# Second joint attention: the samples' decay as one 32 by 128 product for each row group, ahead of the key products

## What is computed

```python
def _fox_attend(q, k, v, cq, ck, qpos, kpos):
    scores = jnp.einsum('bthd,bshd->bhts', q, k).astype(jnp.float32) * SCALE
    scores = scores + jnp.moveaxis(cq, 1, 2)[..., :, None] - jnp.moveaxis(ck, 1, 2)[..., None, :]
    mask = kpos[None, :] <= qpos[:, None]
    p = jax.nn.softmax(jnp.where(mask, scores, NEG_INF), axis=-1)
    return jnp.einsum('bhts,bshd->bthd', p.astype(v.dtype), v)
...
    c_all = jnp.cumsum(logf_all, axis=1)
```

## Time and profile before

| | us |
|---|---|
| median of 3 runs | 3663.12 |
| lowest and highest run | 3660.04, 3667.07 |
| time of the profiled execution | 3663.1 |
| its span, first to last instruction | 3661.3 |
| TensorE matmuls busy in it | 3400.0 |
| mean granted clock of TensorE | 0.967 |

### The profile page before, as it was taken

How to read it: one execution, slowest core, us unless ns; L and a number is a source line. 1 busy time by engine, 2 the same in 40 slices (tenths; PEclk the granted TensorE clock), 3 DMA queues, 4 the chain that set the end, 5 groups by cost and what they waited for, 6 DMA issues and landing times. The chain is left out here.

```text
span 3661.3 us, 62984 instructions
## 1 busy us (share of the span) xinstructions
PE 3400.0 (93%) x25000; PEld 2909.1 (79%) x25000; DVE 1601.0 (44%) x2913; ACT 1123.9 (31%) x2343; POOL 254.6 (7%) x338
## 2 busy tenths in 40 slices
PE   8998699798999999997899799999988999999997
PEld 7876466577999999996789756666567999999996
DVE  5417477463333333335231276666533333333334
ACT  4215255443212112113222145555433121211211
POOL 2310000032000000004000000000013000000003
PEclk9999799999999999998999999999988999999999
DMA  5435598443111111112554498889543111111102
GB/s 171 124 126 182 191 325 320 154 155 115 35 34 57 34 46 34 39 41 92 149 175 126 139 362 310 314 314 319 198 167 121 46 34 34 57 34 46 34 30 102
DMA packets 398384, 493.21 MB, mean 135 GB/s; under 512 B 68464, under 2 KB 250256, under 8 KB 398032
## 3 DMA queue, kind: packets, MB, share of 16 engines
q1 hardware_dynamic: 398176, 490.35, 40.3%
HBM read 407.10 MB, written 84.10 MB: 134 GB/s over the span
## 5 line engine op out<-in xcount | busy, mean ns | idle before, releaser
L2546 DVE TENSOR_TENSOR f_gated<-f_gated,f_up 128x384 f32<-128x384 f32 x132 | 73.1, 554 | 736.1 <-ACT f_gated L2476 736.1
L2570 DVE TENSOR_TENSOR f_y<-f_y,f_down 128x512 f32<-128x512 f32 x396 | 269.5, 686 | 229.4 <-PE f_down L2665 229.3
L2652 PE MATMUL f_gate<-m_ht_hi,f_w_hi 128*128 128x384 f32 x1056 | 355.5, 337 | 12.1 <-DVE f_w_lo L2597 12.1
L2652 PE MATMUL f_gate<-m_ht_lo,f_w_hi 128*128 128x384 f32 x1056 | 355.0, 336 | 0.0
L2652 PE MATMUL f_gate<-m_ht_hi,f_w_lo 128*128 128x384 f32 x1056 | 354.9, 336 | 0.0
L2652 PE MATMUL f_up<-m_ht_hi,f_w_lo 128*128 128x384 f32 x1056 | 352.7, 334 | 0.0
L2652 PE MATMUL f_up<-m_ht_hi,f_w_hi 128*128 128x384 f32 x1056 | 352.7, 334 | 0.0
L2652 PE MATMUL f_up<-m_ht_lo,f_w_hi 128*128 128x384 f32 x1056 | 352.7, 334 | 0.0
L2665 PE MATMUL f_down<-f_wo_hi,f_act_hi 128*128 128x512 f32 x792 | 313.8, 396 | 10.5 <-DVE f_y L2570 9.2
L2665 PE MATMUL f_down<-f_wo_lo,f_act_hi 128*128 128x512 f32 x792 | 309.9, 391 | 0.0
L2665 PE MATMUL f_down<-f_wo_hi,f_act_lo 128*128 128x512 f32 x792 | 309.7, 391 | 0.0
(11 more groups left out here) (396 smaller groups left out, 6677.1 us busy)
## 6 DMA issues: line engine op xcount, KB each, us to landing
jc_kc<-in_cache_c_k SPq DMA_DIRECT2D x64, 1024.0 KB, 10.2
jc_vc<-in_cache_c_v SPq DMA_DIRECT2D x64, 1024.0 KB, 8.8
jb_kc<-in_cache_b_k SPq DMA_DIRECT2D x32, 1024.0 KB, 10.7
jb_vc<-in_cache_b_v SPq DMA_DIRECT2D x32, 1024.0 KB, 9.3
m_raw<-in_w_ffn_in SPq DMA_DIRECT2D x44, 512.0 KB
f_raw<-in_w_ffn_in SPq DMA_DIRECT2D x44, 512.0 KB
f_raw_o<-in_w_ffn_out SPq DMA_DIRECT2D x22, 1024.0 KB, 6.4
m_raw<-x SPq DMA_DIRECT2D x18, 512.0 KB, 4.1
```

The lines of the kernel that those rows point to most:

```text
L2546: dve.tensor_tensor(prod[:, b], silu[:, b], up[:, q, 0:gw], ALU.mult).then_inc(prod_done, 1)
L2570: dve.tensor_tensor(part, part, down[:, half, :], ALU.add).then_inc(added, 1)
L2652: last = pe.matmul(acc[:, q, 0:gw], a[:, s, k, u, :], b[:, k, token], start=(k == 0 and j == 0), stop=(k == KT - 1 and j == 2))
```

## The change

In jc the five products of each tile become four, and ahead of them stands one product for each row group that writes all 128 partitions of its PSUM bank at once, with all of `select` for that row group as weights (32 rows by 128 columns) and the same 512 decays. It starts the accumulation (`start=True`), and the key products of jc no longer do. For jb (`diff` is true) nothing changes.

```diff
--- before.py
+++ after.py
@@ -1536,18 +1536,19 @@
                     if u:
                         pe.wait_ge(scaled, u)
                 pe.wait_ge(s_copied, 4 * u + 2 * pair)
-                for step in range(4 if diff else 5):
+                if not diff:
+                    for a in (2 * pair, 2 * pair + 1):
+                        rows_a = slice(Q * a, Q * a + Q)
+                        pe.matmul(s_ps[:, a % 2], select[rows_a], bias[rows_a, u % 2, 0:bank], start=True, stop=False,
+                                  skip_group_check=True, tile_position=(Q * a, 0))
+                for step in range(4):
                     for c in range(4):
                         for a in (2 * pair, 2 * pair + 1):
                             rows_a, hb = slice(Q * a, Q * a + Q), 4 * c + step
-                            if step < 4:
-                                weights = q_blocks[rows_a, hb // 2, hb % 2]
-                                moving = kc[rows_a, u % 2, 0:parts * per, Q * hb:Q * hb + Q]
-                            else:
-                                weights = select[rows_a, Q * c:Q * c + Q]
-                                moving = bias[rows_a, u % 2, 0:bank].rearrange("p (t r) -> p t r", r=Q)
+                            weights = q_blocks[rows_a, hb // 2, hb % 2]
+                            moving = kc[rows_a, u % 2, 0:parts * per, Q * hb:Q * hb + Q]
                             last = pe.matmul(s_ps[Q * c:Q * c + Q, a % 2].rearrange("p (t r) -> p t r", r=Q), weights, moving,
-                                             start=(step == 0), stop=(step == (3 if diff else 4)), skip_group_check=True,
+                                             start=(diff and step == 0), stop=(step == 3), skip_group_check=True,
                                              tile_position=(Q * a, Q * c))
                 last.then_inc(s_done, 1)
```

## The result

The changed kernel takes 3673.14 us (median of 9 runs, 3667.46 to 3675.98), the kernel before 3664.94 (9 runs, 3659.61 to 3668.57): a ratio of 1.0020, 95% interval 1.0011 to 1.0029, or 8.2 us more where 6.4 were forecast. The profiled execution has a span of 3672.2 us, against 3661.3.

A forecast was written before the change was run, and what follows sets the result against it. TensorE, busy 93% of the span, was taken to bound the kernel. Streaming netted 0 and a second tile shape added 32 x 0.201 = 6.4 us to 3663.1, giving 3669.5 us, range 3661 to 3677.

The forecast's parts named there:

- The bound, and what passes through: In jc: TensorE sets the 34 us unit, so every nanosecond added to a pair is exposed, 32 times.
- Streaming nets 0: In a jc pair: two rounds of decay products removed and two added, 0.857 us each way, netting 0.
- row groups one after the other: Rival, jc's wide products: four rounds, 0.86 + 0.20 = 1.06 us a pair, 33.9 us, 3697; chance 0.08.
- passes block: Rival, jc's wide products: three rounds instead of two, 0.63 us a pair, 20.2 us, 3683; chance 0.07.
- Faster: Rival, jc's wide products: a pass at 1 cycle a column, -0.23 us a pair, -7.2 us, 3656; chance 0.03.
- A second shape costs 0.20 us a pair: In a jc pair: opening and closing are paid twice, for two tile shapes, so 4.45 us becomes 4.65.
- Cheap shape change: Rival, jc's shape change: between 0 and 0.09 us a pair, 0 to 2.9 us, 3663 to 3666; chance 0.08.
- Loads in series: Rival, jc's wide weight loads: second row group's waits for the first's, 0.31 us a pair, 9.9 us, 3673.0; chance 0.09.
- Order costs nothing: In a jc pair: the decay product ahead of the keys adds no wait and no DMA; accumulation flags cost nothing.
- The sum: Over jc: 32 pairs x 0.201 us = 6.4 us on 3663.1, giving 3669.5 us, or +0.18%.
- the clock would stay at 1.00: Sign, in jc: a lower granted clock between 2144 and 2620 us would show the prediction wrong.
- 1.5 us that might absorb a little: In jc: two TensorE stalls of 1.0 and 0.5 us could absorb a little; if they stay, nothing.

The follow-up runs named there:

- experiment 5: The changed kernel without its decay products, so the old keys get no decay: 3640.69 us, ratio 0.9933 to the kernel before.
- Experiment 4: The changed kernel with only the first of each pair's two wide decay products, so half of the old keys get no decay: one run of 3676.81 us.
- experiment 9: The changed kernel with the decay split into high and low float32r parts, added by one float32r product per row group: 3658.87 us, ratio 0.9985 to the kernel before.
- experiment 3: The changed kernel with four 32x64 decay products a pair in place of two 32x128, still ahead of the keys: one run of 3678.08 us.
- experiment 1: The kernel before with its decay products, still on 32x32 tiles, moved ahead of the key products: 3666.68 us, ratio 1.0001.
- experiment 8: The changed kernel run once more, nothing altered: 3670.39 us, ratio 1.0017 to the kernel before.
- experiment 11: The kernel of experiment 9 run once more, nothing altered: 3658.72 us, ratio 0.9982 to the kernel before.
- padding: The changed kernel with 24 empty instructions added to each pair on TensorE's queue: 3748.9 us, ratio 1.0229 to the kernel before.

## Why the prediction was right

**The bound, and what passes through.** Right. TensorE sets the unit: the wait of 0.90 us did not shrink, and experiment 5 showed the same for a pair 0.86 us shorter.

**Streaming nets 0.** Right. Experiment 4 shows that two wide products take the time of one, so 4 rounds (1.06 us in the rivals' terms) never arose; *row groups one after the other* and *passes block* are out: the first passes of both row groups start 0.007 us apart, the second passes 0.533 us behind them. *Faster* is out too: with passes of 0.21 us the second would have started earlier, and of these 0.533 us its load, which starts 0.108 behind the first, explains that much; the 0.425 left are 2.0 cycles a column. To halve it took another type (experiment 9), not another tile.

**A second shape costs 0.20 us a pair.** Right, 0.199. The row it was taken from, two products alternating at 0.201 each, was of the same type and width but another number of rows. That the two agree to 0.002 us is in part luck, since the starts in the earlier trace rows are read to 0.01 us. *Cheap shape change* is out: that the cut by rows stays at 32 saves nothing. *Loads in series* is out: two row groups cost 0.007 us more than one. The closing and the opening that I had only split by argument are seen apart in the records (experiment 3): 0.09 us to close a burst of any width, 0.104 for the first load of 128 columns, 0.052 of 64, 0.025 of 32, and 0.0067 for each further tile. The reason that the prediction gave for 0.20 instead of 0.16, the 128 columns of the first load, is thus right, but only in part: a load of 32 columns costs 0.08 us less, and eight tiles instead of two take 0.04 of that back.

**Order costs nothing.** Right (experiment 1).

**The sum.** 32 x 0.199 = 6.4 us, and each comparison of medians, 8.2 and 5.1, has it inside its interval. A term is missing: the steady unit grew by 0.41 to 0.44 us where two pairs give 0.40. The rest, up to 0.04 a unit, is outside the pairs, and no experiment aimed at it. The forecast that the clock would stay at 1.00 failed in one execution, so one of the signs of being wrong that the prediction named did show, though the 0.20 us a pair does not hang on it (experiment 8). I had counted the stalls of the kernel before as 1.5 us that might absorb a little. Nothing shows that they absorbed anything, they are not fixed, and their idle time is less than their cost: the one of 0.5 us made its pair 1.54 us longer, and the units before are 3.9 us above the steady one in all. In profiled executions of the programs here they cost between 0.4 us (experiment 8) and over 12 (experiment 3). The first comparison's excess over 6.4 us is of that size, but only its profiled execution shows a stall in it.

**What ends the stalls.** No experiment aimed at it, but the traces point to it. They hold every transfer of the DMA queues, also of the one that the profile's page calls instruction.

```profile
q8 instruction: 138, 2.26, 0.3%
```

Its 138 transfers (141 in the kernel before) have 16,384 bytes each, and 62 of 141 fall into the 560 us around this stage. All profiled executions together have 19 stalls of more than 0.4 us between 2140 and 2640 us that nothing shown ends. Each of the 19 ended 1.24 to 1.61 us after such a transfer had landed; a moment picked at random would lie there about one time in 25. And two programs ran once with a stall in the second unit and once without it. In the execution without it the transfer had landed earlier (us from the stage's first wait for the exponential):

| execution | transfer landed | stall |
|---|---|---|
| changed kernel | 8.97 | 8.20 to 10.41 |
| experiment 8, the same program | 5.04 | none |
| experiment 11 | 8.96 | 8.26 to 10.32 |
| experiment 9, the same program | 5.40 | none |

So the second unit stalled when this transfer landed 0.7 us or more after TensorE had come to that place, and not when it landed 3 us ahead. That the transfer brings TensorE's own instructions is an inference from the queue's name and these times.

**Open.** Why such a transfer is late in one execution and not in the next, and what sets its place in the program; padding could not test it. Open too is how much of the missing part of experiment 9 (6.5 and 8.4 us seen, 13.8 expected) is the later first keys and how much is stalls; both stand in its two traces.

## What to carry to other kernels

Count a float32 matmul's time by rounds, columns times passes over what runs side by side, and not by instructions: eight small tiles side by side cost what two wide ones on the same rows and columns cost. Then count the bursts of another shape along TensorE's queue, at 0.16 us (tiles of 32 or 64 columns) to 0.20 us (128 columns) each here, and keep products of one shape together, in whatever order. When an effect is below 0.3% of the kernel, read it from a repeated piece (31 or 32 of 32 pairs that agree to 0.002 us) and use the median only to see that nothing else moved.

## What the runs showed of the hardware that was not expected

- Empty instructions with a semaphore increment are not hidden on TensorE: 24 of them made a pair 1.20 us longer at 2.4 GHz (4.65 to 5.85), 0.05 us each, and in that run the granted clock fell to 1.2 GHz for 64 of 500 us.
- A stall of TensorE of 2.2 us cost 5.3: from 0.4 us before its end the granted clock was down at 1.2 GHz for 6.8 us. In experiment 9 a stall of 1.81 us was followed by a clock of 1.00, in experiment 11 one of 1.54 us at the same place by 3.4 us at 1.2 GHz (units of 35.13 and 36.37 us).
- All 19 stalls of over 0.4 us ended 1.24 to 1.61 us after a transfer of 16,384 bytes on the DMA queue named instruction had landed.
- A burst of tiles of another shape costs 0.09 us to close, 0.0008 us for each column of its first load (0.104 for 128) and 0.0067 us for each further tile side by side, at 2.4 GHz.
- A float32r product of 512 columns on a 32x128 tile leaves one record, float32 two. Two such products side by side take 0.423 us instead of 1.058; less the 0.20 of the burst, an estimate, that is 0.22 us of streaming instead of 0.86.
